# A weight slab rounded inside the gate chain of gated linear attention, and a wait moved to its reader

## The reference

```python
log_a = jax.nn.log_sigmoid((ga @ gla_w_alpha[l] + gla_b_alpha[l]).astype(f32)) / GLA_TAU
b = jnp.cumsum(log_a.astype(f32).reshape(Bsz, N, C, H, dk), axis=2)
b_ref = b[:, :, C // 2 - 1:C // 2]
b_last = b[:, :, C - 1:]
attn = jnp.einsum('bnihk,bnjhk->bnhij', q * jnp.exp(b - b_ref), k * jnp.exp(b_ref - b))
kv = jnp.einsum('bnjhk,bnjhv->bnhkv', k * jnp.exp(b_last - b), v)
o_inter = jnp.einsum('bnihk,bnhkv->bnihv', q * jnp.exp(b), s_prev)
```

## Time and profile before

| what | value |
|---|---|
| median of 3 runs | 1980.67 us (1979.62 to 1981.73) |
| the profiled execution's own time | 1978.91 us |
| its span, first to last instruction | 1977.1 us |
| mean granted TensorE clock | 0.964 of full |
| TensorE busy | 1860.9 us, 94% |
| VectorE busy | 933.3 us, 47% |
| ScalarE busy | 720.7 us, 36% |
| POOL busy | 698.2 us, 35% |
| weight slabs transferred | 280 of 512 KB, 3.6 us from issue to landing |

### The profile page before, as it was taken

One profiled execution on the slowest core, in us unless ns is written; L12 is line 12 of the kernel. 1 busy time (PEld: TensorE's weight loads), 2 busy tenths in 40 slices (PEclk: granted clock), 3 DMA queues, 4 the chain that ended last, 5 costly groups with the idle time before them and its releaser, 6 DMA issues.

```text
span 1977.1 us, 26889 instructions
## 1 busy us (share of the span) xinstructions
PE 1860.9 (94%) x11004; PEld 1610.6 (81%) x11004; DVE 933.3 (47%) x1424; ACT 720.7 (36%) x1034; POOL 698.2 (35%) x290
## 2 busy tenths in 40 slices
PE   5999999999999999997899998889998999999997
PEld 3777777778778888886899998778987899999885
DVE  3455523334366656113545455455667265665202
ACT  4444434332343333223346454322332243333221
POOL 2333333344344444442222222212322334444442
PEclk9999999999999999998899998879998999999999
DMA  4222222223223333331221211111211223333331
GB/s 157 75 75 75 75 86 76 85 86 95 87 75 96 96 96 93 99 94 55 65 65 54 73 56 55 54 33 54 65 44 54 75 75 90 93 90 93 96 96 64
DMA packets 44185, 154.15 MB, mean 78 GB/s; under 512 B 5776, under 2 KB 6032, under 8 KB 44064
## 3 DMA queue, kind: packets, MB, share of 16 engines
q1 hardware_dynamic: 44064, 152.44, 25.4%
HBM read 150.33 MB, written 2.10 MB: 77 GB/s over the span
## 4 chain that ended last, share of the span: by engine, by line
PE 83%; DVE 11%; ACT 4%; issue 1%; SPq 0%; ACTq 0%; DMA 0%; DVEq 0%
PE ps L541 81%; DVE arena L1165 4%; ACT arena L822 2%; PE ps L545 2%; DVE full L1311 1%; DVE u_lo L1162 1%; ACT L827 1%; DVE arena L1528 1%; DVE arena L1402 1%; DVE v_hi L1180 0%; DVE arena L1172 0%; DVE h_res L1357 0%; ACTq L1145 0%; DVE arena L1162 0%; ACT r_bc L822 0%
## 5 line engine op out<-in xcount | busy, mean ns | idle before, releaser
L515 POOL TENSOR_TENSOR w_lo<-w_raw,w_hi 128x1024 fp32r<-128x1024 f32 x280 | 690.2, 2468 | 1229.4 <-ACT w_hi L822 1229.3
L541 PE MATMUL ps<-u_hi,w_hi 128*128 128x264 f32 (+3 forms) x2376 | 661.9, 332 | 41.7 <-DVE u_lo L1162 29.9
L541 PE MATMUL ps<-u_hi,w_lo 128*128 128x264 f32 (+3 forms) x2376 | 651.2, 328 | 0.0
L541 PE MATMUL ps<-u_lo,w_hi 128*128 128x264 f32 (+3 forms) x2376 | 648.8, 327 | 0.0
L541 PEld LDWEIGHTS ps<-u_hi,w_hi 128*128 128x128 f32 (+1 forms) x2376 | 403.6, 193 | 98.1 <-issue 44.4
L541 PEld LDWEIGHTS ps<-u_lo,w_hi 128*128 128x128 f32 (+1 forms) x2376 | 403.1, 192 | 37.5 <-issue 0.8
L541 PEld LDWEIGHTS ps<-u_hi,w_lo 128*128 128x128 f32 (+1 forms) x2376 | 404.2, 192 | 35.8 <-issue 1.0
L822 ACT ACTIVATE w_hi<-w_raw 128x1024 fp32r<-128x1024 f32 x280 | 297.0, 1061 | 203.1 <-PE ps L541 167.5
L1172 DVE SCALAR_TENSOR_TENSOR ffn<-ps,par,ffn 128x512 f32<-128x512 f32 (+2 forms) x176 | 132.1, 750 | 192.6 <-ACT ffn L822 187.4
L822 ACT ACTIVATE arena<-ps 128x512 f32<-128x512 f32 (+6 forms) x210 | 91.8, 488 | 323.1 <-PE ps L541 168.0
L541 PE MATMUL ps<-arena 128*64 128x128 f32 (+9 forms) x1212 | 161.0, 289 | 27.9 <-DVE arena L1165 14.6
(11 more groups left out here) (129 smaller groups left out, 1528.3 us busy)
## 6 DMA issues: line engine op xcount, KB each, us to landing
w_raw<-weights SPq DMA_DIRECT2D x280, 512.0 KB, 3.6
h_res<-xT SPq DMA_DIRECT2D x4, 512.0 KB, 5.2
outT<-h_res SPq DMA_DIRECT2D x8, 256.0 KB, 2.1
cst<-consts SPq DMA_DIRECT2D x1, 992.0 KB, 9.4
par<-params SPq DMA_DIRECT2D x1, 243.5 KB, 6.8
msk<-cmask SPq DMA_DIRECT2D x1, 64.0 KB, 9.4
h_res<-metaT SPq DMA_DIRECT2D x1, 64.0 KB, 8.6
arena<-w_alpha SPq DMA_DIRECT2D x1, 32.0 KB, 9.1
```

What stands on the lines that cost most here:

```text
L515: nc.gpsimd.tensor_tensor(w_lo[:, s % SPL, 0:n], w_raw[:, s % RAW, 0:n], w_hi[:, s % SPL, 0:n], ALU.subtract).then_inc(w_lo_ok, 1)
L541: return nc.tensor.matmul(out, lhsT, rhs, start=start, stop=stop)
```

## The change

In `prep` of GLA, ScalarE now rounds the slab that it would otherwise round at the start of the group `cc` (that is `cb`'s slab, two further on) between the softplus and the exponentials. On VectorE the wait for `st_c` goes from the head of the multiplications to the first instruction that writes `g_qZ`, which is moved behind three others; the link goes with it. In HGRN2 `qz2` is multiplied last, behind the wait for `st_c`; at the old place of that wait there is one for `st_a` (the `head_a` products of the last head), except in HGRN2's first head, which keeps the old one.

```diff
                     f(gt2, x, ACT.Relu, scale=-1.0, bias=negb[:, n:n + 1]).then_inc(sp_ok, 1)
+
+                    split_weights(GROUP_OF[("cc", n)])
                     act.wait_ge(cum_ok, n + 1)
...
                     evacuated(dve, GROUP_OF[("gk", n)])
-                    if n:
-
-                        dve.wait_ge(st_c, n)
...
                     mul(g_kZ[:, :, GLA_C:], k4[:, :, 1, :], eL[:, :, 1, :])
-                    mul(g_qZ[:, :, 0:GLA_C], q4[:, :, 0, :], eB[:, :, 0, :])
                     mul(g_D, d[:, :, 0], d[:, :, 1])
-                    link(mul(g_qB, q4[:, :, 1, :], eB[:, :, 1, :]))
+                    mul(g_qB, q4[:, :, 1, :], eB[:, :, 1, :])
+                    if n:
+
+                        dve.wait_ge(st_c, n)
+                    link(mul(g_qZ[:, :, 0:GLA_C], q4[:, :, 0, :], eB[:, :, 0, :]))
...
                 dve.wait_ge(exp_ok, n + 1)
-                dve.wait_ge(st_c, n)
+                if n == GLA_H:
+
+                    dve.wait_ge(st_c, n)
+                else:
+                    dve.wait_ge(st_a, n)
...
                 mul(h_D, four(h_lead)[:, :, SUB - 1], last_q[:, :, SUB - 1])
-                mul(qz2.rearrange("p b t -> p (b t)").rearrange("p (c t) -> p c t", t=HG_C),
-                    qd2[:, META:T2].rearrange("p (c t) -> p c t", t=HG_C), bc(h_lead, HG_C))
-
                 for c in range(1, SUB + 1):
...
-                last.then_inc(ready, 1)
+
+                dve.wait_ge(st_c, n)
+                mul(qz2.rearrange("p b t -> p (b t)").rearrange("p (c t) -> p c t", t=HG_C),
+                    qd2[:, META:T2].rearrange("p (c t) -> p c t", t=HG_C), bc(h_lead, HG_C)).then_inc(ready, 1)
```

## The result

The changed kernel takes 1987.8 us (median of 9 runs, 1983.55 to 1992.47); the kernel before, beside it, 1980.51 (9 runs, 1978.74 to 1984.39). The ratio is 1.0038 with a 95% interval of 1.0025 to 1.0051: slower by 0.4%. The forecast was a change too small to measure, 2.6 us slower; measured are 7.3. So the measured time lies at rival C's 1989.0 rather than at the forecast's 1983.2. The runs of the changed kernel also lie further apart, 8.9 us against 5.7, and their time goes with TensorE's mean granted clock: 0.964 of full in the run of 1983.55, 0.957 in that of 1992.47.

The account below looks back on a forecast made before the run. TensorE, busy for 94% of the span, was taken as the bound, other engines counting only where it waits. Less 3.2 us for earlier `head_a`, plus 5.8 for the clock, gave 1980.67 + 2.6, rounded to 1983.2; range 1974 to 1988.

Parts of the forecast that it names:

- rival C: GLA heads: the clock stays down through `head_a`, a second slow stretch per head adding 5.8 us: 1989.0; chance 0.15.
- The stall goes, `ready` is next: GLA heads: the 2.28 us stall ahead of `cb` goes; `head_a` instead waits 2.8 us for the multiplications of line 1165.
- A: GLA chain: VectorE's subtractions do not meet POOL; 11.6 us less in four heads, no clock loss: 1969.1; chance 0.12.
- B: GLA chain: the scan lets POOL pass, `ready` 0.78 earlier, clock falls in two or three heads: -2.7, 1978.0; chance 0.18.
- `head_a` earlier by 3.2 us in four heads: GLA heads: `head_a` starts 8.45 us after `cx`, against 9.51, 8.48, 9.5 and 9.5: 3.2 us less.
- The order and the waits cost nothing: VectorE's multiplications, GLA and HGRN2: new order and moved waits change nothing, at worst 0.7 us in seven heads.
- The clock, "I take it in all four, 5.8 us": Behind the waits ahead of `head_a` in GLA: a slow stretch costs 1.44 us per head, 5.8 in all; bounds none and eight.

Follow-up runs that it names:

- e3: The changed kernel with eleven idle 512-column matmuls on TensorE inside the wait for `ready` of each GLA head: 1977.56 us, ratio 0.9984.
- e5: The kernel before with nine idle 512-column matmuls on TensorE ahead of `cb` in each GLA head, inside the 2.28 us stall: 1979.1 us, ratio 0.9988.
- e2: The changed kernel without the earlier rounding of `cb`'s slab, keeping the moved waits and the new order of multiplications: 1980.03 us, ratio 1.0003.
- e1: The kernel before with only `cb`'s slab rounded between softplus and exponentials, VectorE's waits and order as before: 1990.26 us, ratio 1.0041.
- e6: The changed kernel with two idle matmuls ahead of the wait for `ready` in each GLA head: 1983.87 us, ratio 1.0030.
- e8: The changed kernel with `cb`'s slab rounded ahead of the four softplus instructions instead of behind them: 1978.98 us, ratio 1.0003.
- e7: The kernel before with one more 0.6 us ScalarE copy between the exponentials and `cb`'s slab, lengthening the stall: 1982.22 us, ratio 1.0009.
- e4: The changed kernel with ScalarE waiting for `ready` ahead of the slab it rounds in the group `cx`: 1971.29 us, ratio 0.9953.
- e9: The changed kernel with `cb`'s slab rounded ahead of the softplus and ScalarE waiting for `ready` ahead of `cx`'s slab: 1968.96 us, ratio 0.9948.

## Why the prediction was wrong

*The stall goes, `ready` is next.* Right, nearly to the tenth. The wait forecast was 2.8 us for line 1165 in four heads, the profile has 2.84 to 2.86. POOL meets the scan and the first subtraction: forecast 2.06 us late by the row of the feed-forward part, measured 2.02 (2.71 less 0.69). The Trainium skill, page "SBUF — State Buffer", section "Who interferes with whom", has a VectorE instruction with two SBUF inputs contend with a GpSimd instruction that reads SBUF; the scan, which it does not name, has two such inputs, and the profile after agrees, with POOL's 3.16 us. Rivals A and B, in which the scan or the subtractions did not meet POOL, fell with that.

*`head_a` earlier by 3.2 us in four heads.* Right: e3, in which only this is left, is 3.6 us below its kernel before (1981.12), and the interval of e5 holds it. It is no gain from the stall itself: nearly all of it is the clock loss of before, which went.

*The order and the waits cost nothing.* Right: e2, whose HGRN2 waits are those of before, and the same six instructions in 2.75 us in both kernels. (The first instruction that writes `g_qZ` moved behind two others, not three.)

*The clock, "I take it in all four, 5.8 us".* This step failed. That the clock falls in all four heads was right in both profiles with the wait of 2.85 us, and so was the price of a spell as before (1.44 a head). The length was wrong: behind a wait ahead of `head_a` the clock can stay low twice as long or more. The profiled execution has 20.2 us at half clock, at 0.42 each 8.5 us, and e1's had 32.9, or 13.8 us. With 8.5 for 5.8 the sum is +5.3 by the prediction's own steps; the profiled span grew by 7.1, of which 1.5 are the normalisations' waits, which the change does not touch. In the medians the term is 10.2 us (the changed kernel less e3). (1980.67 + 2.6 is 1983.3, not 1983.2, which changes nothing.)

Some evidence had been in the earlier trace rows, where HGRN2's first `head_a` ran at half clock throughout. Rival C took that up and came out nearest, though only in part: in the changed kernel's profile the second slow stretch came in two heads of four, not in all. I gave it 0.15, since HGRN2's matmuls have 32 columns where GLA's have 64, and let the length of the wait decide, beyond 2.28 us. e6 and e8 have long spells behind waits of 2.38 and 1.80 us, and e7 has short ones behind 2.74: where the wait stands decides. That it is the small matmuls behind it is not shown.

## What to carry to other kernels

A stall that goes away is worth what lies between it and the next bound: here the second bound stood 1.1 us behind, and the whole 9.1 us of stall had been worth 3.2, which could be had just as well by keeping TensorE busy in it. Where a wait is moved ahead of small matmuls, allow for a clock that stays down longer than it did behind large ones; here it did in ten falls of twelve. And before a transfer or a rounding is moved for the sake of its consumer, look at which instructions of other engines its helper will meet in the new place: taking POOL off VectorE's chain altogether gave 10 us, moving it along the chain gave nothing (e8) or cost 7 (the change).

## What the runs showed of the hardware that I had not expected

- A wait of 1.8 us ahead of `head_a` (e8) was enough for the clock to fall in two heads of four, while 1.2 us ahead of `head_b` (e4) never was. No shortest wait follows from that: in HGRN2's second head the clock fell behind 0.86 to 0.87 us in e4, e7 and e9, each time to 0.72 over 12 us, and stayed at 1.00 behind the same wait in the profiles before and after.
- The same waits gave 20 us at half clock in one execution and 33 in another (the changed kernel, e1), whose spans differ by 4.7 us.
- The clock stayed at 2.4 GHz through all GLA heads when idle matmuls filled the wait, 10.2 us in the median for eleven matmuls of 0.23 us in each of four heads.
